# Weight loads issued by ScalarE instead of SyncE, and cache copies in rows of at most 4,096 bytes

## The chip, the core and the metric

The kernel runs on one core of a Trainium2 chip, in one launch. The metric is device time in microseconds from launch to end, the median of the runs. The core has TensorE (PE, matmuls), VectorE (DVE), ScalarE (ACT), GpSimd (POOL) and SyncE (SP, which issues DMAs and waits), each with an instruction stream of its own, tied by semaphores. SP, ACT and POOL can each issue DMAs; 16 DMA engines, shared by all, carry them out. Times in profiles are microseconds from the start of the span; "ns" is written where it is nanoseconds.

## The reference

One inference step of a two-layer decoder trunk, for a prompt of 256 tokens and for 8 sequences of 4 new tokens behind 2048 cached ones (288 token columns together). Each layer computes, in float32:

```
xn = rms_norm(x) * norm_w
p  = xn @ w_in                      # 35 tiles of 128 columns
a  = top-k sparse attention (indexer scores over 2048 cached keys, paged K and V)
c  = dilated sliding-window attention (windows 128, 512, 2048; dilations 1, 4, 16)
b  = Mamba-2 SSD branch (causal conv, chunked scan, state of 8 sequences)
h  = x + concat(a * silu(g_a), c * silu(g_c), b) @ w_out     # 8 tiles
```

The outputs are both normalised streams, the new keys and values, the SSD and conv states, and the window caches of each sequence moved on by 4 rows. For the last of these a cache of 128, 512 or 2048 rows is read from HBM and all but its first 4 rows are written to an output: 124, 508 and 2044 KB for each of 8 sequences and 2 layers, a plain copy that nothing in the kernel waits for until its end.

## The kernel before, in words

Everything is feature-major: x is 8 tiles of 128 features by 288 columns. The weights of a layer are 43 tiles of 512 KB (128 partitions by 4 KB), 35 for `w_in` and 8 for `w_out`; `w` in SBUF holds four of them (`WSLOTS`), so tile n + 4 can be loaded once PE has finished tile n. PE computes a tile as 8 products over k, each two instructions in the profile (line 825), into one of two PSUM banks; ACT (`evac`) or DVE (for the first three tiles of a layer, `LATE_ROOT`) moves the result to SBUF. There is no scheduler: each engine's order is written out by hand in its block, and semaphores `filled<bank>` and `drained<bank>` tie a tile's last matmul to its eviction, and that to the next use of the bank (`bank_plan`).

The layer goes through stages that the profile shows well:

- start: sum of squares of x, tiles 0 to 7.
- page stage: 16 page pairs (`page_pair`), each from two ring slots, with tiles 8 to 15 in between. A page load (`kv<-in_kk`) has 128 rows of 1,280 bytes.
- copy stage: tiles 16 to 26, between them the counting passes of the top-k threshold on DVE (`hit`) and the SSD heads. POOL issues the 24 cache copies here (`keep`), three after each of the tiles 16 to 21, 23 and 24.
- value stage: tiles 27 to 34 with windows (`kv<-in_dil`, 576 KB) and value pages (`kv<-in_vv`, 128 rows of 1,024 bytes).
- output: the 8 tiles of `w_out`, then the next layer's sum of squares.

Pages, windows and values pass through a ring of eight slots of `kv`. Loads of even places of the ring are issued by SP, of odd places by POOL, each when PE has used the item eight places before (`load_item`, line 404 for pages, 397 for windows). SP also issues every weight load (`load_w`, line 425), in `next_w(i)`: it waits until tile i is filled, then loads tile i + 4. SP's program interleaves these with the ring's loads in the order in which PE will release them. ACT issues no DMA. POOL's DMAs go through the queue that the profile calls q0, software_dynamic, SP's through q1, hardware_dynamic.

Of the kernel before, what the change touches and what calls it, by code (L numbers as in the profile page):

```python
# [23 lines left out]
DEPTH = 2  # L24
# [185 lines left out]
def build(nc, a):  # L210

    plan, _ = bank_plan()
    with ExitStack() as ctx:
# [103 lines left out]
        def filled(use):  # L317
            return S[f"filled{plan[use][0]}"]
# [101 lines left out]
        def _(sync):  # L420
            SP = mybir.EngineType.SP

            def load_w(layer, i):
                n = layer * NW + i
                sync.dma_start(w[:, n % WSLOTS, :, :].rearrange("p k n -> p (k n)"),
                               a["w"][n // NW, n % NW]).then_inc(S[f"w_in{n % WSLOTS}"], 16)

# [3 lines left out]
            load_w(0, 0)  # L431
            sync.dma_start(ptab[:, :], a["ptab"]).then_inc(S["ptab_in"], 16)
            load_w(0, 1)
            load_w(0, 2)
            sync.dma_start(const[:, :], a["const"]).then_inc(S["const_in"], 16)
            load_w(0, 3)
# [6 lines left out]
            for L in range(DEPTH):  # L443

                def next_w(i):


                    n = L * NW + i + WSLOTS
                    if n < DEPTH * NW:
                        use = f"proj{i}" if i < NTILE else f"out{i - NTILE}"  # L450
                        sync.wait_ge(filled(use), nth(L, use))
                        load_w(0, n)

# [5 lines left out]
                for i in range(8):  # L459
                    next_w(i)  # L460
                for u in range(NPAIR):
                    consumed(("page", 2 * u), ("page", 2 * u + 1))
                    if u % 2 == 1:
                        next_w(8 + u // 2)
# [3 lines left out]
                for i in range(16, 27):  # L468
                    next_w(i)
                for i, (lo, hi) in enumerate(((32, 40), (40, 44), (44, 46), (46, 54), (54, 62), (62, 66), (66, 70), (70, 74))):  # L470
                    consumed(*RING[lo:hi])
                    next_w(27 + i)
                consumed(*RING[74:])
                for m in range(KT):
                    next_w(NTILE + m)
# [7 lines left out]
        def _(pool):  # L483
# [5 lines left out]
            for L in range(DEPTH):  # L489
                ly = bass.ds(L, 1)  # L490

                def keep(b, use):

                    pool.wait_ge(filled(use), nth(L, use))
                    for g in range(3):
                        pool.dma_start(a[f"keep{g}"][ly, b], a[f"buf{g}"][ly, b, 4 * 256:]).then_inc(S["copied"], 16)  # L496
# [75 lines left out]
        def _(act):  # L572
            act.wait_ge(S["ones_set"], 1)
# [19 lines left out]
            for L in range(DEPTH):  # L593
                chain = Chain(S["act_chain"])

                def evac(i):
# [18 lines left out]
                    else:  # L615
                        act.activation(ptile(i), src[:, 0:T], fn).then_inc(use, 1)  # L616

# [74 lines left out]

                if L == 0:
# [119 lines left out]
                for k in range(KT):  # L813
                    square(L + 1, k)
# [1377 lines left out]
```

## Time and profile before

| | |
|---|---|
| runs | 687.83, 688.44, 694.17 us; median 688.44 |
| span of the profiled execution | 683.4 us, first to last instruction |
| that execution's own time | not given beside its span; the median of the runs lies 5.0 us above the span |
| PE busy | 614.2 us, 90% of the span |
| DVE, ACT, POOL busy | 377.5, 167.9, 224.5 us |
| DMA | 198.38 MB, mean 290 GB/s |
| mean granted TensorE clock | 0.957 of full |
| weight loads | 86 of 512 KB, 7.6 us to landing in the median |
| cache copies | 48: 16 each of 124, 508 and 2044 KB |

The page gives each engine's busy time, a strip of 40 slices, the chain of work that ended last, the costliest groups of instructions, and for each kind of DMA the median time from issue to landing. A PE wait is attributed to what released it; a chain of waits gives the whole length of a transfer, however much of it lies beside other work. A DMA's share is that of the 16 engines' time; it can come out a little over 1 in a short stretch, since a packet counts where it starts.

### The profile page before, as it was taken

To read this page: it belongs to the slowest core of one execution; us is meant where nothing else is said; L and a number is where in the kernel's file an instruction comes from. 1 tells how busy PE (TensorE), PEld (TensorE's weight loads), DVE (VectorE), ACT (ScalarE), POOL (GpSimd) and SP (SyncE) were. 2 spreads that over 40 slices of the span, in tenths; PEclk is the share of its full clock that TensorE was granted. 3 is DMA by queue.
4 is the path that set the end of the run, shared out by engine and by line. 5 is a ranking of instruction groups with operands and counts; after the bars stand their busy time and mean duration, and the time that the engine had idled before them with its cause. 6 is when DMAs were issued, how large, how long until landed. Compare 5 with 4: busy or idle time off the path is not lost.

```text
span 683.4 us, 13785 instructions
## 1 busy us (share of the span) xinstructions
PE 614.2 (90%) x4870; PEld 428.3 (63%) x4870; DVE 377.5 (55%) x1150; ACT 167.9 (25%) x405; POOL 224.5 (33%) x406
## 2 busy tenths in 40 slices
PE   6899999898989978979999999988899997898994
PEld 3676565565667755647777665566656775565772
DVE  3754655777759535433147475577766953543213
ACT  3015322121113202550111352312211320235111
POOL 2207540242106675451000475123120667541000
PEclk9999999998889998999999999999989999799897
DMA  8939999999978899995333799999998889993111
GB/s 333 374 133 315 367 369 408 418 346 356 350 246 270 308 315 371 351 293 204 113 115 141 263 369 369 395 408 376 367 361 297 276 307 310 371 332 121 54 69 69
DMA packets 67766, 198.38 MB, mean 290 GB/s; under 512 B 11537, under 2 KB 40370, under 8 KB 66418
## 3 DMA queue, kind: packets, MB, share of 16 engines
q1 hardware_dynamic: 49682, 99.99, 41.6%
q0 software_dynamic: 18016, 97.50, 39.7%
q8 instruction: 39, 0.64, 0.4%
q14 instruction: 29, 0.24, 0.1%
HBM read 189.30 MB, written 52.00 MB: 353 GB/s over the span
## 4 chain that ended last, share of the span: by engine, by line
PE 57%; DMA 18%; DVE 14%; SPq 4%; ACT 4%; issue 3%; DVEq 0%; ACTq 0%
PE bank L825 55%; DMA w<-in_w 6%; DMA kv<-in_kk 6%; DMA kv<-in_vv 5%; SPq L404 3%; DVE hit L1452 3%; PE bank L875 2%; DVE tb L1465 1%; DVE st L1954 1%; DMA ptab<-in_ptab 1%; ACT srow L766 1%; ACT shared L663 1%; DVE shared L1575 1%; ACT shared L680 1%; DVE tb L1463 1%
## 5 line engine op out<-in xcount | busy, mean ns | idle before, releaser
L825 PE MATMUL bank<-xn,w 128*128 128x288 f32 x1120 | 304.2, 426 | 4.7 <-DMA w<-in_w 4.7
L825 PEld LDWEIGHTS bank<-xn,w 128*128 128x128 f32 x1120 | 212.3, 197 | 78.4 <-issue 17.4
L404 POOL DMA_DIRECT2D kv<-in_kk x128 | 68.8, 538 | 153.6 <-issue 98.1
L404 POOL DMA_DIRECT2D kv<-in_vv x160 | 86.4, 540 | 99.3 <-PE bank L825 72.7
L616 ACT ACTIVATE pt<-bank 128x288 f32<-128x288 f32 x48 | 19.6, 409 | 237.7 <-PE bank L825 237.7
L825 PE MATMUL bank<-pt,w 128*128 128x288 f32 x256 | 65.2, 410 | 0.0
L825 PEld LDWEIGHTS bank<-pt,w 128*128 128x128 f32 x256 | 48.8, 192 | 14.1 <-issue 0.7
L496 POOL DMA_DIRECT2D out_keep<-in_buf x48 | 23.5, 495 | 81.3 <-PE bank L825 73.3
L825 PE MATMUL bank<-kv,pt 128*32 128x256 f32 x512 | 38.2, 406 | 11.5 <-DMA kv<-in_vv 11.3
L1452 DVE TENSOR_SCALAR_CACHE_REDUCE hit<-sc,tb 128x516 bf16<-128x516 f32 x62 | 46.5, 750 | 2.2
L2022 DVE TENSOR_TENSOR x<-x,bank 128x288 f32<-128x288 f32 x16 | 7.3, 454 | 50.2 <-PE bank L825 50.1
L825 PE MATMUL bank<-kv,qz 128*32 128x256 f32 x512 | 34.3, 385 | 0.0
L1463 DVE TENSOR_SCALAR tb<-bank 128x1 int32<-128x1 f32 x62 | 9.5, 154 | 42.5 <-PE bank L825 42.1
L1425 DVE COPY tails<-cin 128x3 f32<-128x3 f32 x14 | 7.2, 512 | 41.3 <-ACT cin L614 39.1
L825 PEld LDWEIGHTS bank<-cnt,seg 128*128 128x128 f16 x68 | 6.7, 100 | 35.9 <-issue 34.0
L825 PE MATMUL bank<-cnt,seg 128*128 128x1 f16 x68 | 11.1, 168 | 19.5 <-DVE hit L1452 18.8
L825 PEld LDWEIGHTS bank<-kv,pt 128*32 128x32 f32 x512 | 13.9, 112 | 22.4 <-DMA kv<-in_vv 10.1
L583 ACT ACTIVATE phased<-x 128x288 f32<-128x288 f32 x24 | 10.5, 442 | 70.6 <-DVE x L2022 67.6
L825 PE MATMUL bank<-kv,shared 128*32 128x128 f32 x768 | 26.6, 283 | 0.0
L825 PE MATMUL bank<-pt 64*128 64x128 f32 (+3 forms) x168 | 26.3, 334 | 0.0
L518 POOL TENSOR_SCALAR xwb<-xws,const 32x384 f32<-32x384 f32 x16 | 21.6, 1354 | 13.4 <-DVE xws L1715 7.6
L825 PEld LDWEIGHTS bank<-pt 64*128 64x128 f32 (+2 forms) x168 | 17.9, 183 | 10.6 <-issue 9.8
(238 smaller groups left out, 802.8 us busy)
## 6 DMA issues: line engine op xcount, KB each, us to landing
w<-in_w SPq DMA_DIRECT2D x86, 512.0 KB, 7.6
out_keep<-in_buf POOLq DMA_DIRECT2D x16, 2044.0 KB, 14.3
kv<-in_kk SPq DMA_DIRECT2D x128, 160.0 KB, 8.8
kv<-in_kk POOLq DMA_DIRECT2D x128, 160.0 KB, 5.8
kv<-in_vv POOLq DMA_DIRECT2D x160, 128.0 KB, 5.3
kv<-in_dil SPq DMA_DIRECT2D x24, 576.0 KB, 8.2
kv<-in_vv SPq DMA_DIRECT2D x96, 128.0 KB, 5.1
out_keep<-in_buf POOLq DMA_DIRECT2D x16, 508.0 KB, 8.8
```

Source lines behind the costliest of these rows:

```text
L404: engine.dma_start(kv[:, s, r * rec:(r + 1) * rec], a["kk" if what == "page" else "vv"][bass.ds(page + layer * N_POOL, 1)].rearrange("o p ...
L496: pool.dma_start(a[f"keep{g}"][ly, b], a[f"buf{g}"][ly, b, 4 * 256:]).then_inc(S["copied"], 16)
L518: pool.tensor_scalar(xwb[:, b % 2, :], xws[0:32, 2, :], C("bm", b, b + 1, slice(0, 32)), None, ALU.mult).then_inc(S["xwb_ready"], 1)
L583: act.activation(squares[:, k % 2, 0:T], x[:, k, :], ACT.Square).then_inc(S["sq_ready"], 1)
L616: act.activation(ptile(i), src[:, 0:T], fn).then_inc(use, 1)
L663: act.activation(psa[:, i, 0:nk], psa[:, i, 0:nk], ACT.Exp, bias=st8[:, 1, i:i + 1], accum_out=st8[:, 2, i:i + 1]).then_inc(S["pexp"] if i ...
L825: return pe.matmul(out, lhsT, rhs, start=start, stop=stop, skip_group_check=True, **k)
L875: return pe.transpose(out, in_, ident(n))
L1425: dve.tensor_copy(tails[:, n, 0:3], cin[:, n % 2, TP:TP + 3]).then_inc(chain.next(), 1)
L1452: ts_(hit[:, :], sc[:, :], old.bitcast(F32), 0.0, ALU.is_ge, ALU.add, accum_out=cnt[:, 0:1]).then_inc(S["cnt_ready"], 1)
L1463: ts_(tb[:, 2:3], src[:, 0:1], float(TOPK_S), float(bit), ALU.is_lt, ALU.mult).then_inc(drained(f"count{n}"), 1)
L2022: tt_(x[:, m, :], x[:, m, :], src[:, 0:T], ALU.add).then_inc(drained(f"out{m}"), 1)
```

## The change

ACT issues all weight loads. The first four come before anything else in its program; the next three behind the first root, and each later one directly behind the eviction of the tile whose slot it refills (`next_w(i)` at the end of `evac(i)`; for the output tiles ahead of `square`). SP keeps x, the parameters, the constants, the even places of the ring and the state. The copies get `max_dma_last_dim=4096`, which cuts each into equal rows of at most 4,096 bytes.

```diff
@@ block.sync
-            def load_w(layer, i):
-                n = layer * NW + i
-                sync.dma_start(w[:, n % WSLOTS, :, :].rearrange("p k n -> p (k n)"),
-                               a["w"][n // NW, n % NW]).then_inc(S[f"w_in{n % WSLOTS}"], 16)
-
             for n in range(2):
                 sync.dma_start(x[:, 4 * n:4 * n + 4, :], a["x"][:, 4 * n:4 * n + 4, :]).then_inc(S[f"x_in{n}"], 16)
             sync.dma_start(prm[:, :, :], a["prm"]).then_inc(S["prm_in"], 16)
-            load_w(0, 0)
             sync.dma_start(ptab[:, :], a["ptab"]).then_inc(S["ptab_in"], 16)
-            load_w(0, 1)
-            load_w(0, 2)
             sync.dma_start(const[:, :], a["const"]).then_inc(S["const_in"], 16)
-            load_w(0, 3)
...
-                for i in range(8):
-                    next_w(i)
                 for u in range(NPAIR):
                     consumed(("page", 2 * u), ("page", 2 * u + 1))
-                    if u % 2 == 1:
-                        next_w(8 + u // 2)
...
-                for i in range(16, 27):
-                    next_w(i)
-                for i, (lo, hi) in enumerate(((32, 40), (40, 44), (44, 46), (46, 54), (54, 62), (62, 66), (66, 70), (70, 74))):
-                    consumed(*RING[lo:hi])
-                    next_w(27 + i)
-                consumed(*RING[74:])
-                for m in range(KT):
-                    next_w(NTILE + m)
+                consumed(*RING[32:])
@@ block.gpsimd, keep(b, use)
-                        pool.dma_start(a[f"keep{g}"][ly, b], a[f"buf{g}"][ly, b, 4 * 256:]).then_inc(S["copied"], 16)
+                        pool.dma_start(a[f"keep{g}"][ly, b], a[f"buf{g}"][ly, b, 4 * 256:], max_dma_last_dim=4096).then_inc(S["copied"], 16)
@@ block.scalar
+            def load_w(n):
+
+                act.dma_start(w[:, n % WSLOTS, :, :].rearrange("p k n -> p (k n)"),
+                              a["w"][n // NW, n % NW]).then_inc(S[f"w_in{n % WSLOTS}"], 16)
+
+            for n in range(WSLOTS):
+                load_w(n)
             act.wait_ge(S["ones_set"], 1)
...
+                def next_w(i):
+
+                    n = L * NW + i + WSLOTS
+                    if n < DEPTH * NW:
+                        use = f"proj{i}" if i < NTILE else f"out{i - NTILE}"
+                        act.wait_ge(filled(use), nth(L, use))
+                        load_w(n)
...
                     else:
                         act.activation(ptile(i), src[:, 0:T], fn).then_inc(use, 1)
+                    next_w(i)
...
+                for i in range(LATE_ROOT):
+                    next_w(i)
...
                 for k in range(KT):
+                    next_w(NTILE + k)
                     square(L + 1, k)
```

SP at the start of the program, before, from its second instruction on; `w<-in_w` is a weight tile, `x`, `prm`, `ptab`, `const`, `cst`, `bconst` and `fnw` are the other first loads:

```order
L429 DMA x<-in_x 128x1152 x2
L430 DMA prm<-in_prm 128x102
L425 DMA w<-in_w 128x1024
L432 DMA ptab<-in_ptab 1x256
L425 DMA w<-in_w 128x1024 x2
L435 DMA const<-in_const 128x1844
L425 DMA w<-in_w 128x1024
L437 DMA cst<-in_conv 128x336
L439 DMA bconst<-in_bconst 128x1932
L439 DMA fnw<-in_fnw 128x8
L400 TENSOR_LOAD ptab
```

The same place of SP in the change:

```order
L424 DMA x<-in_x 128x1152 x2
L425 DMA prm<-in_prm 128x102
L426 DMA ptab<-in_ptab 1x256
L427 DMA const<-in_const 128x1844
L428 DMA cst<-in_conv 128x336
L430 DMA bconst<-in_bconst 128x1932
L430 DMA fnw<-in_fnw 128x8
L400 TENSOR_LOAD ptab
```

ACT at the start of the program in the change (`phased` holds the squares, `pt` the evicted tiles); before, it had the same rows without the DMAs:

```order
L542 UNCONDITIONAL_BRANCH
L546 DMA w<-in_w 128x1024 x4
L561 ACT_TABLE_LOAD
L561 ACTIVATE phased<-x 128x288 x8
L566 ACT_TABLE_LOAD
L566 ACTIVATE rstd<-bank,eps 128x288
L546 DMA w<-in_w 128x1024 x3
L602 ACTIVATE pt<-bank 128x288
L546 DMA w<-in_w 128x1024
L591 ACTIVATE misc<-bank 64x288
L592 ACTIVATE pt<-bank 64x288
L546 DMA w<-in_w 128x1024
```

The four first weight tiles have moved from between SP's loads to the head of ACT's program, the next three behind the root (`rstd`), and the others each behind the eviction of its tile.

SP in the middle of the page stage, before, where one page item ends and the next begins; `ptab` is the load of page numbers into registers:

```order
L404 ISA
L404 DMA kv<-in_kk 128x320
L404 ISA
L404 DMA kv<-in_kk 128x320
L404 ISA
L404 DMA kv<-in_kk 128x320
L425 DMA w<-in_w 128x1024
L400 TENSOR_LOAD ptab
L404 ISA
```

ACT behind the eviction of tile 28, in the change (`vtok` are the turned value tiles, of which PE waits for `drained`):

```order
L602 ACT_TABLE_LOAD
L602 ACTIVATE pt<-bank 128x288
L546 DMA w<-in_w 128x1024
L643 ACTIVATE vtok<-bank 128x384 x2
L643 ACTIVATE vtok<-bank 32x384
L771 ACTIVATE shared<-bank 128x32x2 x3
L775 ACTIVATE ea<-bank 32x384
```

On SP the weight load between two page items is gone, so that only page loads follow each other; on ACT a weight load now stands between an eviction and what followed it directly.

POOL at the first `keep`, before:

```order
L397 DMA kv<-in_dil 128x1152 x4
L513 DMA out_tails<-tails 128x189
L496 DMA out_keep<-in_buf 16x1984
L496 DMA out_keep<-in_buf 16x8128
L496 DMA out_keep<-in_buf 32x16352
L500 DMA out_feat<-pt 128x288
L500 DMA out_feat<-pt 128x576
```

The same in the change:

```order
L397 DMA kv<-in_dil 128x1152 x4
L484 DMA out_tails<-tails 128x189
L467 DMA out_keep<-in_buf 32x992
L467 DMA out_keep<-in_buf 128x1016
L467 DMA out_keep<-in_buf 512x1022
L471 DMA out_feat<-pt 128x288
L471 DMA out_feat<-pt 128x576
```

The order is the same; the three copies have 32, 128 and 512 rows of 3,968, 4,064 and 4,088 bytes where they had 16, 16 and 32 rows of 7,936, 32,512 and 65,408. (The order's rows count elements of 4 bytes.)

## Rows read from the trace of the kernel before

**Rows 1.** the page: busy us, share of the span, instructions, by engine

```profile
PE 614.2 (90%) x4870; PEld 428.3 (63%) x4870; DVE 377.5 (55%) x1150; ACT 167.9 (25%) x405; POOL 224.5 (33%) x406
```

**Rows 2.** busy us in stretches: page stage, both layers' starts, copy stage

```profile
49.50:116.40 66.90, 65.40 (x693) 39.19 (x693) 37.07 (x118) 23.93 (x61) 31.01 (x54) 1.00 1.01 360
13.10:53.00 39.90, 35.98 (x218) 26.46 (x216) 25.27 (x76) 5.18 (x13) 8.63 (x18) 1.00 0.72 257
344.30:381.50 37.20, 36.65 (x221) 27.26 (x220) 25.61 (x76) 6.16 (x14) 0.56 (x2) 1.00 0.37 129
121.50:198.50 77.00, 66.42 (x382) 47.29 (x383) 53.63 (x203) 14.16 (x43) 18.27 (x40) 0.93 1.00 363
```

**Rows 3.** the waits of PE: us in total, times, longest

```profile
PE bank L825 <- DMA kv<-in_vv: 11.3, 8, 2.9
...
PE bank L825 <- DMA w<-in_w: 4.7, 2, 3.4
PE bank L825 <- DMA kv<-in_kk: 2.3, 4, 0.9
PE bank L875 <- ACT vtok L656: 1.4, 4, 0.5
PE bank L875 <- ACT pt L773: 1.3, 4, 0.4
...
PE bank L825 <- ACT relun L700: 1.1, 2, 0.6
```

**Rows 4.** chain of waits, end of the copy stage: start, us, what

```profile
163.77 34.05 DMA w<-in_w
...
197.86 6.00 PE bank L825 x18
```

**Rows 5.** tile x: the two loads' issues, and us from issue to landing

```profile
L429 SPq DMA_DIRECT2D x<-in_x x2: 391/406/421, 0.9 to 1.3; - x2
...
DMA to landing us min/median/max: 3.8/4.3/4.8
```

**Rows 6.** SP's timeline at the start: when the seven next weight loads begin

```profile
21.92 23.34 SPq L425 DMA_DIRECT2D w<-in_w  x7
```

**Rows 7.** PE's timeline at the start

```profile
32.19 8.03 PE L825 MATMUL bank<-xn,w 128*128 128x288 f32 x32 [3.37 <-DMA w<-in_w]
```

**Rows 8.** DMA queues between 81 and 83: packets, MB, share of 16 engines

```profile
q0 software_dynamic: 152, 0.52, 73.0%
q1 hardware_dynamic: 160, 0.21, 31.2%
```

**Rows 9.** chain of waits of the page stage: start, us, what

```profile
95.26 13.64 DMA kv<-in_kk
```

**Rows 10.** SP's timeline in the page stage: start, us, what

```profile
97.30 0.34 SPq L425 DMA_DIRECT2D w<-in_w  x1
...
105.19 0.33 SPq L425 DMA_DIRECT2D w<-in_w  x1
```

**Rows 11.** DMA queues between 158 and 175: packets, MB, share

```profile
q0 software_dynamic: 219, 5.15, 83.4%
q1 hardware_dynamic: 219, 0.77, 14.4%
```

**Rows 12.** stretches as in rows 2, PE alone

```profile
198.00:201.40 3.40, 3.40 (x8) 0.50 0.49 182
201.40:210.00 8.60, 8.35 (x170) 1.00 0.28 94
524.00:529.00 5.00, 4.75 (x26) 1.00 0.47 166
```

**Rows 13.** PE's timeline in the second layer's value stage

```profile
595.79 1.07 PE L825 MATMUL bank<-kv,pt 128*32 128x256 f32 x16 [1.90 <-DMA kv<-in_vv]
```

**Rows 14.** all weight loads: issue ns min/median/max, then us to landing

```profile
L425 SPq DMA_DIRECT2D w<-in_w x86: 327/328/1615, 2.3 to 654.3; - x86
...
DMA to landing us min/median/max: 3.3/7.6/34.0
```

More of the change, by code:

```diff
@@ L443, in _ @@
             for L in range(DEPTH):
[L445 to L452, printed above, removed]
                 def consumed(*items):
```

## The prediction, made before the change was run

> **What bounds the kernel now.** I read the page first: TensorE (PE) is busy 614.2 us of the 683.4 us span, in 4870 matmuls, and no other engine comes near [rows 1]. The change touches no matmul and no eviction, so it can only move PE's idle time, some 69 us, and the clock that PE is granted. Next the busy time by stage [rows 2]: a row has the stretch, its length, the busy us of PE, weight loads, DVE, ACT and POOL with counts, the granted clock, the DMA engines' share and GB/s. In the page stage (49.5 to 116.4) PE idles 1.5 us of 66.9, with the DMA engines at 1.01: PE and DMA are both full. The copy stage (121.5 to 198.5) again has DMA at 1.00, while PE idles for other reasons. Then the waits of PE [rows 3]: 11.3 us for value pages (kv<-in_vv), 4.7 us for weights, 2.3 us for key pages (kv<-in_kk). The 86 weight loads cost PE 4.7 us in all, though the chain of waits puts one of 34.05 us on the path [rows 4]: that row is the length of a transfer, 33 us of it beside PE's own work. So what the weights can win is small, and what the other loads can lose by sharing must be weighed against it.
>
> **Term 1, the first loads.** SP's queue had x, the parameters and then four weight tiles; now ACT issues the four tiles at once, beside x. The two halves of x (576 KB each) are issued 0.9 and 1.3 us in and land 3.8 and 4.8 us later [rows 5], so at 4.7 and 6.1: the second takes 1.4 us at the full rate. If the weights take every second turn, the first half needs 1.4 us more. PE's first sum of squares waits for it, and the first tiles follow. I take **+1.4 us**; bounds 0 (x gets ahead) and +2.9 (both halves late and both on the path).
>
> **Term 2, tile 4.** Its load stood on SP behind 16 page loads and left at 21.92 [rows 6]; PE was ready at 28.8 and waited 3.37 us for it [rows 7]. On ACT it leaves once tile 0 is filled, three tiles of 4.0 us before that, near 17, and has over 10 us to land. The whole wait is not won: DVE and ACT then become the next. The second layer's same eight tiles have no such wait and take 37.2 us where the first takes 39.9 [rows 2]. I take the difference, **-2.7 us**; bounds -3.4 and -1.0.
>
> **Term 3, the page stage.** Here the queue matters. Between 81 and 83 the software queue (POOL) had 152 packets and 0.52 MB, the hardware queue (SP) 160 packets and 0.21 MB [rows 8]: they alternate packet by packet, and the bigger packet gets the bigger share. SP's pages of 1,280-byte rows are the losers. In SP's own queue the weights stood in line with them; from a queue of their own, with 4 KB packets, they take a turn in each round, ahead of pages that were issued earlier. The last SP page load leaves at 95.26 and lands 13.64 us later, and PE goes on with it [rows 9]. Two weight loads leave meanwhile, at 97.30 and 105.19 [rows 10]; before, they stood behind that page. Now the first, 512 KB at the 360 GB/s of this stage [rows 2], puts 1.5 us in front of it, the second, with some 2 us of its transfer left, a third of a share, 0.6 us at most. The engines were full already, so the page lands later by that. I take 1.6 us a layer, the first load and little of the second: **+3.2 us** for both layers. Bounds: -2.3 (the waits for pages vanish) and +4.0.
>
> **Term 4, the copy stage.** The cache copies moved in pieces of up to 65,408 bytes, and now move in pieces of at most 4,096. Between 158 and 175 each queue had 219 packets, the copies 5.15 MB, the weights 0.77 MB [rows 11]: one for one again. Each engine has 8 weight rows of a tile, and each waits for one copy packet. That is why the load of tile 26 took 34.05 us and PE started on it only at 197.86 [rows 4]. With equal packets it should land in some 6 us. The wait was 4.7 less 3.37, so 1.3 us. Behind it the clock fell to 0.50 for 3.4 us [rows 12], the lower of its levels, 1.2 GHz; the same tile of the second layer, with no wait ahead, kept 1.00. Half of 3.4 us is 1.7. **-3.0 us**, all in the first layer; bounds -3.0 and 0 (the threshold count on DVE is next on this path, and the clock can fall elsewhere).
>
> The Trainium skill speaks against this term: its page "DMA: Bandwidth & Descriptors", section "Queues, rings and completion order", has a DMA engine drain a whole packet of typically 9 to 17 descriptors from one row's ring before it turns to the next. By that all 8 rows of a weight tile would pass behind a single copy packet, the copies' size would not matter, and the sum would be 3.0 us higher, 693.1. The trace's 219 to 219 and the 34 us disagree with it.
>
> **Term 5, the copies themselves.** 24 copies a layer, 21.9 MB. In the first window above the copies had 83.4% of 16 engines over 17 us for 5.15 MB, 22.7 GB/s an engine; POOL's small packets [rows 8] make 22.2, SP's 21.0. So smaller rows make 60 us of copying 1 to 5 us longer, which lies in the stretch after 201.4, where the engines are at 0.28 [rows 12]: **0**. If that room were gone, up to 5 us a layer would appear at the value pages. POOL's issue instructions may grow; its pages wait for PE there, not for POOL.
>
> **Term 6, the value stage.** PE waits 11.3 us for value pages [rows 3], and the last wait of the second layer, 1.90 us, is for an SP load [rows 13]. Tile 35's load leaves in front of it and now competes. One load is worth 1.5 us, as in term 3; part of it has no time to interfere. I take 0.6 us a layer, **+1.2 us**; bounds 0 and +3.0.
>
> **Term 7, ACT's issues.** An issue takes SP 327 ns at least, 328 in the median, 1,615 at most [rows 14]. ACT makes 82 behind evictions; the eviction itself is not delayed, what comes after it on ACT is. PE waits for such work at `relun`, for the turned weights `pt` and for `vtok` [rows 3], eight places in all where a new issue lies just before. Bounds: 0 (the issue runs while ACT still computes) and 8 x 0.33 = +2.6. I take 0.2 each, **+1.6 us**.
>
> **Sum:** 1.4 - 2.7 + 3.2 - 3.0 + 0 + 1.2 + 1.6 = +1.7 us against the profiled execution. Its span is 683.4 us; the median, 688.44, lies 5.0 above it, which nothing here changes. Forecast **690.1 us**.
>
> **Rivals.**
>
> *The queue is neutral.* Weights on ACT's queue take nothing from the pages; they only leave the line in front of them. For it: POOL's share can shrink instead of SP's. Against it: the alternation in [rows 8]. Then term 3 is -1.5 and term 6 is 0: 1.4 - 2.7 - 1.5 - 3.0 + 1.6 = -4.2, so 684.2 us. The same page of the skill, section "Issuing engines are not separate DMA queues", says that issuing from another engine saves only the sequencer's time; by that rule it would be this case.
>
> *ACT is held by its issues (slower).* SP's issues reach 1,615 ns where its queue is deep. If ACT's meet that at the eight places of term 7, each costs 1.3 us instead of 0.2: +8.8, so 698.9 us. It decides from about 1 us an issue. Against it: ACT has at most four loads in flight, SP up to sixteen.
>
> *The copies overrun (slower).* If a 4 KB packet between two places of HBM took 1.5 times its share, the copying would last 30 us longer, POOL's value pages would stand behind it in the same queue, and after some 20 us of room PE would wait 10 us a layer: 710 us. It needs 1.35 times; the nearest rows say 1.08 at most.
>
> *The value stage speeds up too (faster).* SP's queue loses its heaviest rows, the waits for in_vv [rows 3] shrink by a third, and a spell of half clock as the first in [rows 12] goes in each layer: the neutral case less 3.8 and less 2 x 1.7, so 677 us.
>
> **Chances.** The forecast's mechanisms 0.50, with their own range of 686 to 695; the neutral queue 0.28; ACT held 0.08; copies overrun 0.05; value stage faster 0.06; something else 0.03. The forecast's low bounds and the neutral case set the low end, 683.0; term 3 at its upper end, the upper bounds of 1, 6 and 7 and most of the held ACT set the high end, 697.5. Outside lie the fast rival, the overrun and the tails, 0.2 together. About 1%, 6.9 us, is what a measurement of this kernel can tell from no change. Faster than 681.6: the fast rival and a tail of the neutral case, 0.13. Slower than 695.3: both slow rivals and a tail of the forecast, 0.20. Within: 0.67.
>
> **What the profile of the changed kernel would show.** Term 1: the second half of x lands near 9 instead of 6.1, tile 0 starts near 14.5. Term 2: no wait of PE at tile 4. Term 3: page-stage weights land in 5 to 7 us, SP's last pages later than 13.64 us after issue, and PE's waits for in_kk above 2.3 us; if they are gone, the neutral rival holds. Term 4: no weight load over 12 us, tile 26 without a wait and at full clock. Term 5: small packets in q0, its last copy before 207. Term 7: waits for `relun`, `pt` and `vtok` 0.2 us longer each. What would make the forecast wrong is a stage whose time moves by more than 3 us, above all the value stage, or spells of half clock that come or go without a wait beside them.

## The result, and the profile after

The changed kernel takes **800.02 us** (median of 4 runs, 796.93 to 803.46), the kernel before 691.11 us beside it: a ratio of 1.157, 95% interval 1.150 to 1.165. 690.1 was forecast, with a range up to 697.5. The prediction was wrong by 110 us. A kernel's runs fall into a faster and a slower state of the chip, some per cent apart: times here are medians of all runs, ratios compare fast runs only, and of the profiled executions those of experiments 16, 17 and 18 were slow ones.

The profiled execution has a span of 795.3 us against 683.4. Busy time by engine, from the page, to set beside [rows 1]:

```profile
PE 628.7 (79%) x4870; PEld 435.9 (55%) x4870; DVE 378.2 (48%) x1150; ACT 169.7 (21%) x405; POOL 228.1 (29%) x406
```

The instructions are the same, and only PE's busy time grew, by 14.5 us. The rest is waiting. PE's waits, with total, times and longest (compare [rows 3]):

```profile
PE bank L815 <- DMA kv<-in_vv: 93.8, 13, 28.3
...
PE bank L815 <- issue: 8.4, 4, 4.6
...
PE bank L815 <- DMA kv<-in_kk: 6.5, 5, 1.8
PE bank L815 <- DMA w<-in_w: 5.1, 2, 3.8
PE bank L865 <- ACT pt L762: 2.5, 3, 1.1
PE bank L865 <- ACT vtok L643: 1.7, 4, 0.5
PE bank L815 <- ACT relun L689: 1.1, 2, 0.5
```

The waits for value pages grew from 11.3 to 93.8 us, 82.5 of the 111.9 us. With PE's extra busy time and the 8.4 us of "issue" (waits that end in nothing the profile shows) that makes 105. Four waits are 79.4 of the 93.8 us, on PE's timeline (start, length, what, and in brackets the idle time ahead):

```profile
254.74 1.08 PE L815 MATMUL bank<-kv,pt 128*32 128x256 f32 x8 [18.31 <-DMA kv<-in_vv]
284.12 1.94 PE L815 MATMUL bank<-kv,pt 128*32 128x256 f32 x16 [28.30 <-DMA kv<-in_vv]
635.74 1.08 PE L815 MATMUL bank<-kv,pt 128*32 128x256 f32 x8 [11.96 <-DMA kv<-in_vv]
657.65 1.94 PE L815 MATMUL bank<-kv,pt 128*32 128x256 f32 x16 [20.84 <-DMA kv<-in_vv]
```

The issues of these pages began in time, at 212.9 (207.5 before). These are the loads issued from 214 to 223, with the median time to landing:

```profile
kv<-in_vv POOLq DMA_DIRECT2D x12, 128.0 KB, 48.7
kv<-in_vv SPq DMA_DIRECT2D x8, 128.0 KB, 33.8
```

Before, the median over all such loads was 5.3 us on POOL's queue and 5.1 on SP's. Both queues are late, not only POOL's, in which the copies stand. The page that POOL issued at 217.5 landed 66.6 us later, at 284.1, where the longest of the four waits ends; SP's of 215.2 landed 39.4 us later, at 254.6, where the wait of 18.31 us ends. What is ahead of them are the copies of the first layer, last issued at about 187: ns of an issue and the first and last issue, then us from issue to landing:

```profile
L467 POOL DMA_DIRECT2D out_keep<-in_buf x48: 503/532/631, 121.8 to 585.1; - x48
...
DMA to landing us min/median/max: 4.2/49.2/94.3
```

Before, the median was 10.8 us and the longest 23.8. The last copy of the first layer was issued at 187.0 and took the 94.3 us, so it landed at 281.3, and 3 us later the longest wait of PE ends. Stretches as in [rows 2] (us, busy us by engine, granted clock, DMA share, GB/s) show it from both sides:

```profile
49.50:116.40 66.90, 63.42 (x656) 38.04 (x655) 35.43 (x114) 24.04 (x61) 31.02 (x54) 1.00 1.01 363
13.10:53.00 39.90, 39.27 (x229) 29.02 (x230) 25.89 (x78) 7.56 (x17) 10.07 (x19) 1.00 0.77 265
121.00:198.00 77.00, 65.97 (x366) 46.33 (x364) 52.20 (x199) 14.98 (x43) 19.73 (x40) 0.91 1.06 211
198.00:240.00 42.00, 28.29 (x307) 21.98 (x306) 23.69 (x69) 8.45 (x15) 12.04 (x19) 0.77 1.02 209
240.00:300.00 60.00, 15.11 (x90) 8.95 (x91) 2.99 (x6) 2.55 (x8) 7.18 (x10) 0.57 0.67 202
```

Up to 116 the kernels agree within 2 us. In the copy stage PE still does its work (65.97 of 77 us), and the DMA engines are as full as before (1.06), but they move **211 GB/s where they moved 363** [rows 2]. A full engine with 60% of its bytes is the sign to look for: its packets take longer, though not all of them. The trace's packet records, which the views only sum, show which: between 130 and 190 half of ACT's weight packets of 4,096 bytes took 159 ns, in the change as in experiment 3 below, but the slowest tenth took 995 ns and more for 170, and the mean was 386 for 173. Of the copies' packets of 8,176 bytes the median was 455 ns, the mean 696 and the slowest tenth over 1,478; in experiment 6, with packets of the same size, 311, 374 and 521. So a part of the packets is held up for long, and that part makes most of the loss. The bill comes after 198. Of 234.1 to 292.1, which lies around the two waits, PE computes 9.78 us, at the lower clock throughout:

```profile
234.10:292.10 58.00, 9.78 (x48) 5.23 (x49) 3.41 (x16) 3.13 (x6) 4.62 (x9) 0.50 0.74 219
```

Last, the DMA queues from 158 to 175, to set beside [rows 11] (packets, MB, share of 16 engines; q10 is ACT's):

```profile
q0 software_dynamic: 266, 1.90, 62.7%
q10 hardware_dynamic: 261, 0.97, 43.4%
```

The copies' 1.90 MB in 62.7% of 16 engines over 17 us are 11.1 GB/s an engine, against 22.7 before: 2.04 times the time for a byte. ACT's weight rows, at 8.2 GB/s an engine, suffer too, though their rows are 4,096 bytes as before.

### The profile page after: what moved, and what is told of

It is laid out like the page before. It is cut to its first block, busy times and chain, and to the rows that moved or that the text cites. A ratio compares the mean times of both kernels' runs of the same rounds, so it can differ in the third digit from the quotient of the medians.

```text
span 795.3 us, 13785 instructions
## 1 busy us (share of the span) xinstructions
PE 628.7 (79%) x4870; PEld 435.9 (55%) x4870; DVE 378.2 (48%) x1150; ACT 169.7 (21%) x405; POOL 228.1 (29%) x406
## 4 chain that ended last, share of the span: by engine, by line
PE 54%; DMA 25%; DVE 9%; another core or an unknown queue 4%; issue 3%; ACT 2%; SPq 2%; POOLq 0%; DVEq 0%; ACTq 0%; POOL 0%
PE bank L815 52%; DMA kv<-in_vv 14%; DMA kv<-in_kk 5%; DMA w<-in_w 5%; DVE hit L1442 2%; PE bank L865 2%; SPq L404 2%; DVE tb L1455 1%; DMA x<-in_x 1%; ACT shared L650 1%; DVE shared L1565 0%; ACT shared L667 0%; DVE st L1571 0%; DVE tb L1453 0%
## 5 line engine op out<-in xcount | busy, mean ns | idle before, releaser
L815 PE MATMUL bank<-xn,w 128*128 128x288 f32 x1120 | 310.6, 433 | 5.1 <-DMA w<-in_w 5.1
L815 PEld LDWEIGHTS bank<-xn,w 128*128 128x128 f32 x1120 | 216.7, 201 | 82.2 <-issue 19.0
L815 PE MATMUL bank<-kv,pt 128*32 128x256 f32 x512 | 42.4, 436 | 93.8 <-DMA kv<-in_vv 93.8
L404 POOL DMA_DIRECT2D kv<-in_kk x128 | 69.1, 540 | 158.0 <-issue 94.4
L1754 DVE TENSOR_TENSOR phased<-phased,ebc 128x384 f32<-128x384 f32 x16 | 9.0, 560 | 115.1 <-PE bank L815 115.1
L467 POOL DMA_DIRECT2D out_keep<-in_buf x48 | 26.5, 557 | 82.2 <-PE bank L815 80.4
L815 PE MATMUL bank<-kv,shared 128*32 128x128 f32 x768 | 31.1, 307 | 8.2 <-issue 8.2
L815 PEld LDWEIGHTS bank<-kv,shared 128*32 128x32 f32 x768 | 24.9, 124 | 13.4 <-issue 11.0
L815 PEld LDWEIGHTS bank<-cnt,seg 128*128 128x128 f16 x68 | 6.7, 101 | 35.8 <-issue 33.8
## 6 DMA issues: line engine op xcount, KB each, us to landing
kv<-in_vv SPq DMA_DIRECT2D x96, 128.0 KB, 11.1
```

The source lines that it names most:

```text
L404: engine.dma_start(kv[:, s, r * rec:(r + 1) * rec], a["kk" if what == "page" else "vv"][bass.ds(page + layer * N_POOL, 1)].rearrange("o p ...
L815: return pe.matmul(out, lhsT, rhs, start=start, stop=stop, skip_group_check=True, **k)
L1754: tt_(state[:, b, :].rearrange("p (h n) -> p h n", h=6), state[:, b, :].rearrange("p (h n) -> p h n", h=6), each(ebc[:, :, 2 + b], 64), AL ...
```

## The experiments

The rate of the DMA engines between 130 and 190, in the first layer's copy stage, is the common measure: the engines are full there (share 0.98 to 1.07) in every kernel. It is the last number of the row of that stretch. In every experiment whose time stays under 710 us the same stretch of the second layer, 460 to 520, gives the same within 7 GB/s. Experiments 3 and 16 have the same copies and gave 368 and 357, so a difference of 11 between two kernels is not read as one. The last column is the ratio of times to the kernel before, which ran beside each experiment anew (medians of 687.8 to 691.1 us), with its 95% interval.

| | copy pieces | starts off a 32-byte multiple | GB/s | us | ratio |
|---|---|---|---|---|---|
| before | 65,408 | none | 355 | | 1 |
| change | 4,088 end to end | 3 of 4 | 199 | 800.0 | 1.157 (1.150, 1.165) |
| 1 | 65,408, old copies | none | 358 | 690.9 | 1.006 (1.002, 1.010) |
| 2 | 4,088, weights on SP | 3 of 4 | 225 | 779.3 | 1.136 (1.127, 1.145) |
| 3 | 4,096 | none | 368 | 689.6 | 1.003 (0.998, 1.008) |
| 4 | 65,400 | 3 of 4 | 338 | 690.2 | 1.005 (1.001, 1.009) |
| 5 | 4,032 | none | 362 | 688.0 | 1.004 (1.000, 1.009) |
| 6 | 4,088, 8 bytes apart | none | 356 | 689.5 | 1.005 (1.000, 1.010) |
| 7 | 4,096, read at +8 | reads only | 363 | 693.6 | 1.014 (1.004, 1.023) |
| 8 | 4,096, written at +8 | writes only | 312 | 701.0 | 1.025 (1.016, 1.034) |
| 9 | 4,096, both at +8 | all | 306 | 701.2 | 1.017 (1.014, 1.021) |
| 10 | 4,104 end to end | 3 of 4 | 221 | 788.7 | 1.142 (1.138, 1.146) |
| 11 | 4,032, both at +8 | all | 331 | 694.6 | 1.008 (1.003, 1.012) |
| 12 | 4,064 | none | 364 | 689.8 | 0.999 (0.994, 1.004) |
| 13 | 4,096, both at +24 | all | 305 | 706.3 | 1.023 (1.015, 1.031) |
| 14 | 4,080 | 1 of 2 | 334 | 697.4 | 1.013 (1.007, 1.020) |
| 15 | 8,184 | 3 of 4 | 328 | 699.2 | 1.017 (1.010, 1.024) |
| 16 | as 3, first weights on SP | none | 357 | 687.1 | 0.999 (0.995, 1.004) |
| 17 | 4,088, 8 bytes apart, both at +8 | all, no shared unit | 357 | 690.3 | 0.999 (0.994, 1.005) |
| 18 | 4,088, read apart, written end to end | writes only, 3 of 4 | 220 | 782.6 | 1.129 (1.116, 1.142) |

The piece of 4,088 bytes is what a limit of 4,096 makes of a cache of 2,093,056 bytes: 512 equal pieces of 8 x 511. The smaller caches got 4,064 and 3,968. The trace shows the sizes: packets of 8,176 bytes, two rows each. Within its tensor every cache begins at a multiple of 4,096 bytes. "Starts off a 32-byte multiple" is counted from there, for the largest cache, on the written side where nothing else is said; the other two caches hold a quarter of the bytes, and in the change their rows of 4,064 and 3,968 bytes are multiples of 32.

**Experiment 1: the weights alone.** The changed kernel with the old copies.

```diff
-  pool.dma_start(a[f"keep{g}"][ly, b], a[f"buf{g}"][ly, b, 4 * 256:], max_dma_last_dim=4096)
+  pool.dma_start(a[f"keep{g}"][ly, b], a[f"buf{g}"][ly, b, 4 * 256:])
```

> Weight loads on ACT as in the change, copies in their old pieces of up to 65,408 bytes. Theories that blame the copies (their piece size, or where the pieces start) expect the other terms of the forecast alone: first loads +1.9 (measured in the changed kernel), tile 4 -2.7, pages +3.2, values +1.2, issues 0.3, so near 693 us, between 686 and 697, with the last copy of layer 0 landed before 200 us and the loads of the copy stage taking up to 34 us as before. The theory that a queue of ACT's own for the weights is what slows the DMA engines expects over 740 us and copies that land after 240 us.

690.93 us. A queue of ACT's own is not the cause of the loss. This kernel carries the other terms of the forecast and is read for them below.

**Experiment 2: the copies alone.** The kernel before with only the edit of the copies.

> Weight loads on SP as before, copies in pieces of at most 4,096 bytes (4,088 in fact). Both theories of the copies expect the whole loss: 800 us, 785 to 815, copies landing near 280 us. The theory of ACT's queue expects 688 to 700 us.

779.31 us. The edit of the copies is the cause. That it is 20 us less than the whole change is more than the other terms give; with ACT's loads beside them the copies move at 199 GB/s, with SP's at 225.

**Experiment 3: 4,096 bytes exactly.** Same size within 8 bytes, other borders.

```diff
+  keep, buf, n = a[f"keep{g}"][ly, b], a[f"buf{g}"][ly, b, 4 * 256:], (WINS[g] - 4) * 256
+  m = 1024
+  r = n // m // 16 * 16
+  for lo, hi, k in ((0, r * m, r), (r * m, n, 16)):
+      pool.dma_start(keep[:, lo:hi].rearrange("o (k e) -> o k e", k=k), buf[:, lo:hi].rearrange("o (k e) -> o k e", k=k), max_dma_last_dim=4096)
```

> The changed kernel with the same bytes copied in pieces of 4,096 bytes, each of which starts at a multiple of 4,096 (the last 61,440 bytes of each cache in 16 pieces of 3,840), in place of 4,088. Theory alignment (4,088 is 8 x 511, so nearly every piece begins and ends inside a 64-byte line, and the partial lines cost): near the kernel of experiment 1, 690 to 700 us. Theory piece size (any piece near 4 KB between two places of HBM is dear): 785 to 815 us. In between, 720 to 760, would mean that both count.

689.61 us: the whole loss is gone with 8 bytes more in a piece, so pieces near 4 KB are not dear as such. The copies' queue between 158 and 175, as above:

```profile
q0 software_dynamic: 1465, 5.23, 84.7%
q10 hardware_dynamic: 292, 1.05, 16.1%
```

That is 22.7 GB/s an engine, the same as with 65,408 bytes. Nor does any weight load stand behind a copy now (ns of an issue, then us to landing; before the longest was 34.0, [rows 14]):

```profile
L550 ACTq DMA_DIRECT2D w<-in_w x86: 333/334/983, 0.9 to 654.8; - x86
...
DMA to landing us min/median/max: 3.3/6.5/12.2
```

**Experiment 4: large pieces at odd places.** 65,400 bytes in place of 65,408.

> Weight loads on ACT; copies in large pieces that start at odd places: 65,400 bytes for the largest cache in place of 65,408 (8 x 8,175), 32,496 and 7,920 for the others, the few bytes left over in 16 small pieces. Theory piece size: as experiment 1, within 3 us. Theory alignment by edges (a price for each piece's two ends): a sixteenth of the loss, 7 us over experiment 1. Theory alignment of the whole piece (every burst of a displaced piece is split): 750 us and more.

690.21 us: 20 GB/s less than with 65,408 in the stage (340 for 358 in the second layer too), nothing in the time. That rules out a price by the byte, and it fits a price at the borders, of which there are a sixteenth.

**Experiments 5, 12 and 14: the grid.** Pieces of 4,032, 4,064 and 4,080 bytes end to end, written as in experiment 3 with m = 1008, 1016, 1020; the starts are multiples of 64, 32 and 16.

> The changed kernel with copy pieces of 4,032 bytes (63 x 64), the rest of each cache in 16 pieces, all starts and lengths multiples of 64 bytes but not of 128. Two such rows make one packet, as with 4,088 bytes. Theory partial 64-byte lines: as the 4,096-byte pieces, 686 to 695 us. Theory that a larger unit counts (128 to 512 bytes, or the 4,096 itself), or that the pairs of rows in a packet are what is dear: 740 us and more.

> Pieces of 4,064 bytes (127 x 32), two rows a packet, undisplaced: every second start lies 32 bytes inside a 64-byte line, the others on it. If 64-byte lines count, half of the borders are unaligned against 7 of 8 with 4,088 bytes: 4/7 of the 110 us, near 750 us. If the unit is 32 bytes: 686 to 695 us.

> Pieces of 4,080 bytes (255 x 16), two rows a packet, undisplaced: starts drift over 0, 16, 32, 48 in a line. If only starts that are no multiple of 16 are dear: 686 to 695 us. If the unit is 32 bytes, half of the starts are off it, against three quarters with 4,088: about 760 us (2/3 of the loss). If the drift is what counts, whatever the unit: 760 to 800.

362, 364 and 334 GB/s. Multiples of 64 and of 32 are free, those of 16 lose 8%, with half of the borders inside a 32-byte unit. So the unit is 32 bytes, not the 64 that the expectation of experiment 3 named. But 4,080 costs far less than two thirds of the loss.

**Experiments 6 and 17: off the grid, but no unit shared.** Pieces of 4,088 bytes at a stride of 4,096, with the 8 bytes left out at the end (6) or at the start (17). The lines are those of 6; in 17 both sides begin 8 bytes further, and the last 61,184 bytes of the largest cache go end to end in 16 pieces of 3,824.

```diff
+  dst = keep[:, lo:lo + k * m].rearrange("o (k e) -> o k e", k=k)[:, :, 0:used]
+  src = buf[:, lo:lo + k * m].rearrange("o (k e) -> o k e", k=k)[:, :, 0:used]
```

> Pieces that start at multiples of 4,096 bytes, but only the first 4,088 of each are copied (8 of 4,096 bytes are left out), so every piece ends inside a line, and no line is written by two pieces. Theory of the partial line by itself (the memory has to read and merge it): half of the partial lines are left, so half of the loss or more, 730 to 800 us. Theory of the shared line (two pieces, on two DMA engines, write the same line at about the same time and wait for one another): 686 to 695 us.

> The mirror of experiment 6: pieces of 4,088 bytes at a stride of 4,096 on both sides, each starting 8 bytes behind a multiple of 4,096 and ending on one (8 of 4,096 bytes, and 256 bytes of each cache, are left out). No line is shared by two pieces. Theory that the dear pieces are those whose start and end lie differently (every second one with 4,088 bytes packed): under 250 GB/s in the copy stage and 760 us and more. Theory shared lines: 350 GB/s or more, 686 to 695 us. Theory of a fixed price for a start off the grid: 305 to 330 GB/s, 695 to 706 us.

356 and 357 GB/s, what experiment 16 gives with aligned pieces, and no change of the time. A piece with one end inside a unit costs nothing that can be measured, where one of the theories put it at half of the loss or more. Both kernels keep the stride of 4,096 bytes, so they take away the wandering of the starts together with the shared unit, and none of these pieces has both ends inside a unit.

**Experiments 7, 8 and 9: which side.** Pieces of 4,096 bytes, displaced by 8 bytes in the reads, the writes, or both. The lines are those of 8.

```diff
+  dst = keep[:, lo + 2:lo + 2 + k * m].rearrange("o (k e) -> o k e", k=k)
+  src = buf[:, lo + 0:lo + 0 + k * m].rearrange("o (k e) -> o k e", k=k)
```

> Pieces of 4,096 bytes written at multiples of 4,096, read from 8 bytes further (so the copied caches are displaced by 8 bytes, and the last 1,024 bytes of each stay out). Theory that the writes are what costs: 686 to 695 us. Theory that reads at odd places cost: most of the 110 us.

> The mirror of the last: pieces of 4,096 bytes read at multiples of 4,096 and written 8 bytes further (displaced, last 1,024 bytes left out). Theory of the writes: two pieces share a line at every border, as in the changed kernel, with 496 borders in place of 512: 785 to 810 us. Theory of the reads: 686 to 695 us.

> Pieces of 4,096 bytes read and written 8 bytes behind a multiple of 4,096 (the first 8 and the last 1,016 bytes of each cache are left out). Reading alone displaced gave 693.6 us, writing alone 701.0, the changed kernel 800. Theory that the two sides add: near 705 us. Theory that a piece displaced on both sides is what is dear: 780 us and more. Theory that it is the drift of the starts over all places in a line, or the two rows in a packet, which this kernel has not: up to 710 us.

363, 312 and 306 GB/s. Displaced reads do not slow the stage; the time of experiment 7, 1.4% up in four runs (interval 0.4 to 2.3%), is not explained by its rate, and whether it is a loss stays unclear. Displaced writes, where each border now lies inside a unit that two pieces write, take 15 to 17%. The stretch 130 to 190 of experiment 9:

```profile
130.00:190.00 60.00, 53.35 (x301) 37.76 (x301) 42.16 (x159) 12.31 (x35) 26.01 (x54) 0.91 1.04 306
```

PE's 53.35 us there are as good as the 53.12 of experiment 3 and the 51.95 of the change: it is not this stage that shows the damage. The theory of the writes had put experiment 8 at 785 us or more, and it measured 84 less: a shared unit at every border is not yet what the change has.

**Experiments 10 and 11: wandering starts, or two rows in a packet.** 4,104 bytes end to end (one row a packet), and 4,032 bytes all displaced by 8 (two rows a packet).

> Pieces of 4,104 bytes (8 x 513), one row a packet, whose starts drift by 8 bytes from row to row as those of the changed kernel do the other way. Theory drift: near 800 us. Theory that two rows in a packet of the queue are what is dear together with odd starts: 700 to 715 us.

> Pieces of 4,032 bytes (63 x 64), two rows a packet, all of them displaced by the same 8 bytes on both sides (the first 8 and up to 248 last bytes of each cache are left out). Undisplaced they gave 688.0 us. Theory that two rows in a packet with odd starts are dear (the line between the two rows of one packet is written twice by one engine in quick succession): 780 to 800 us. Theory drift: 700 to 715 us.

221 and 331 GB/s. Two rows in a packet are not what is dear; starts that wander by 8 bytes, in pieces of this length, are.

**Experiment 13: 24 bytes in place of 8.**

> As experiment 9, with a displacement of 24 bytes in place of 8 on both sides (the first 24 and the last 1,000 bytes of each cache are left out). If every place off the 32-byte grid costs the same, as with 8 bytes: 695 to 705 us. If the place counts, and those deeper in a unit are the dear ones: 760 us and more. If neither, the drift itself is what is dear (neighbouring pieces with different remainders), and this gives 695 to 705 too.

305 GB/s, as with 8. Of these two places within the unit, neither is dearer.

**Experiment 15: pieces twice as long, still wandering by 8 bytes.**

> Pieces of 8,184 bytes (8 x 1,023) for the two larger caches: the same drift of 8 bytes, half as many borders. A price for each piece: half the extra time of the DMA engines, and since the stage has some 20 us of room a layer before PE waits, 700 to 745 us. A price by the byte (a displaced piece moves slower throughout): 780 us and more.

328 GB/s and 699.2 us: not a price by the byte. But neither is it a fixed price for each border: half the borders of experiment 10 give back 90 of its 100 us, and 107 of the 147 GB/s that it lacks to experiment 3.

**Experiment 18: wandering writes, fixed reads.**

```diff
+  dst = keep[:, 0:r * 1022].rearrange("o (k e) -> o k e", k=r)[:, :, 0:1022]
+  src = buf[:, 0:r * 1024].rearrange("o (k e) -> o k e", k=r)[:, :, 0:1022]
```

> Pieces of 4,088 bytes read at a stride of 4,096 from multiples of 4,096, and written end to end at a stride of 4,088 (so they are displaced, and 8 of 4,096 bytes are left out). Theory that the drift of the written places alone is what is dear: 199 to 230 GB/s in the copy stage, 770 to 800 us. Theory that the read side is needed too, or that both must drift together: 300 GB/s and more, under 710 us.

220 GB/s, 782.6 us. The writes alone are enough for nearly all of the loss.

**Experiment 16: the change without its loss, first loads in their old order.** The first four weight tiles go back to SP behind x; the copies are those of experiment 3.

> Aligned pieces of 4,096 bytes and the weights on ACT, but the first four weight tiles on SP behind x, in the order of the kernel before. It takes term 1 out (tile 0 of the first layer started 2.2 us later in experiments 1 and 3). Expected 2 us under experiment 3: a ratio to the kernel before of 0.995 to 1.002, so no change that can be measured; anything under 0.990 would mean that the lateness of x costs more than its 2.2 us.

687.11 us, 0.999 (0.995, 1.004). No version here beats the kernel before by more than can be measured.

**What is shown, and what is open.** Shown: the loss comes from the borders between the written pieces. With borders at multiples of 32 bytes it is gone (3, 5, 12, 16), with 8 bytes between pieces at a stride of 4,096 too (6, 17); where the copies read from does not matter to the rate (7, 18). Fixed borders inside a 32-byte unit that two pieces write cost 9 to 17% of the rate (11 beside 5, 9 and 13 beside 3), and half as many, at starts that wander by 16 bytes, 8% (14 beside 5). That it takes the unit shared by two neighbours, and not a partly written unit alone, is shown for fixed borders only as far as 6 and 17 go: no kernel here has both ends of a piece inside a unit without a neighbour in it. Open: why borders that wander in steps of 8 bytes cost 37% and more with pieces near 4 KB (2, 10, 18, the change), more than twice what fixed ones do, though fewer of them lie inside a unit, and why the same wandering costs only 11% with pieces of 8,184 bytes (15 beside 3) and 6% with 65,400 (4 beside 1). In all of these the pieces also share units; no kernel has wandering starts with gaps between the pieces, so that the shared unit is needed for this large part of the loss is argued and not shown. Lengths that are an odd multiple of 8 do not explain it by themselves (6 and 17 have them). That two DMA engines have to take turns for the unit they share fits all of this, and it fits the long tail of the packets, but no run shows which engine writes which piece.

## Why the prediction was wrong

**Term 5 failed**: "smaller rows make 60 us of copying 1 to 5 us longer", which it then put at 0. It measured 110 us: 800.0 for 689.6 in experiment 3, where only the cutting of the copies differs. From its first issue to its last landing the copying of the first layer took 159.5 us for 76.9. It was costed from the rates of the nearest rows, 22.7 GB/s an engine for the large copy pieces and 21 to 22 for page loads of 1,280-byte rows [rows 8, 11]. For size that was right: with 4,096 bytes the copies run at 22.7. But size was not what counts. The pieces of 4,088 bytes stood in the section on the change, and I did not ask where such pieces begin. None of the rows that I priced by could show it: the large copy pieces, of 7,936, 32,512 and 65,408 bytes, are all multiples of 32, and pages land in SBUF, each row in a partition of its own, while these copies tile one stretch of HBM end to end. The measured rate was 11.1 GB/s an engine.

The unit of 32 bytes stands in the Trainium skill, on its page "Collectives: The Full Stack", section "Rules for kernel authors": buffers, there those of collectives, are to be aligned to 32 bytes, to avoid a read-modify-write by the hardware. Experiments 5, 12 and 14 agree with the unit, by 362 and 364 GB/s for 334. But in experiments 6 and 17, with one partly written unit a piece and 356 and 357 GB/s, such a write costs nothing that can be measured.

**The room behind the copies** was judged rightly, and it decides the size of the loss. In the rival "the copies overrun" I put it at some 20 us a layer. In experiment 9, at 306 GB/s, the copying takes 20 and 16 us longer in the two layers than before, from first issue to last landing, and PE's waits for value pages grow only from 11.3 to 15.3 us in both together. In the change the copying takes 83 us longer in the first layer and 56 in the second, and the same waits grow by 50 and 32: some 33 and 24 us were free. In times: experiments 8, 9 and 13, at 305 to 312 GB/s, lose 1.7 to 2.5%; 14 and 15, at 334 and 328, lose 1.3 and 1.7%; the change, at 199, loses 15.7%. Of the 1.3 to 2.5% the waits for value pages show only a part (10.5 to 17.5 us in these five, 11.3 before); no run says where the rest lies.

That rival had the chain from the copies to the waits, but not the cause: it blamed the 4 KB packet, which experiment 3 clears. It needed 1.35 times the share and got 2.04. It was priced at 30 us of overrun, where the copying took 83 and 56 us longer, and at 10 us a layer, where PE waited 46.6 and 32.8 us in the four rows above. It also took only POOL's queue to be held; SP's value pages took 33.8 us too. What it left out is the clock: 14.5 us more busy time for the same 4,870 matmuls, at a mean granted clock of 0.892 for 0.957. With 0.05 for it, the chance was far too low for a price that no row of the trace bounded from above: the row that I took as the upper bound differed from the new operation in where it writes.

The other terms are read from experiment 1, whose span is 682.6 us against 683.4. PE's timeline at the start of tiles 0, 8, 16 and 27 of the first layer, then of tiles 8, 16 and 27 of the second:

```profile
15.29 0.41 PE L815 MATMUL bank<-xn,w 128*128 128x288 f32 x1
51.48 0.51 PE L815 MATMUL bank<-xn,w 128*128 128x288 f32 x1
115.87 0.51 PE L815 MATMUL bank<-xn,w 128*128 128x288 f32 x1
210.67 0.51 PE L815 MATMUL bank<-xn,w 128*128 128x288 f32 x1
380.73 0.51 PE L815 MATMUL bank<-xn,w 128*128 128x288 f32 x1
444.91 0.51 PE L815 MATMUL bank<-xn,w 128*128 128x288 f32 x1
539.35 0.51 PE L815 MATMUL bank<-xn,w 128*128 128x288 f32 x1
```

The kernel before has, at the same places:

```profile
13.13 0.41 PE L825 MATMUL bank<-xn,w 128*128 128x288 f32 x1
52.96 0.51 PE L825 MATMUL bank<-xn,w 128*128 128x288 f32 x1
116.36 0.51 PE L825 MATMUL bank<-xn,w 128*128 128x288 f32 x1
212.24 0.51 PE L825 MATMUL bank<-xn,w 128*128 128x288 f32 x1
381.51 0.51 PE L825 MATMUL bank<-xn,w 128*128 128x288 f32 x1
444.20 0.51 PE L825 MATMUL bank<-xn,w 128*128 128x288 f32 x1
536.86 0.51 PE L825 MATMUL bank<-xn,w 128*128 128x288 f32 x1
```

- **Term 1** (+1.4): tile 0 starts 2.2 us later, within the bounds, and PE's first wait, for the squares of x, is 8.6 us for 6.7.
- **Term 2** (-2.7): from tile 0 to tile 8 it took 39.83 us and takes 36.19, so -3.6, a little beyond the bound of -3.4. PE has no wait for a weight tile there.
- **Term 3** (+3.2): from tile 8 to tile 16, 63.40 and 62.69 us became 64.39 and 64.18, +2.5 in both layers together. The weights do take turns from the pages: tile 15 of the first layer lands 6.5 us after its issue for 13.3 before, PE's waits for in_kk grow from 2.3 to 4.8 us, by the same 2.5, and the longest is 2.6 us for 0.9. They grow in experiment 3 and in the change too, to 5.3 and 6.5. The neutral rival, by which they do not grow, is wrong here.
- **Term 4** (-3.0): in experiment 1 nothing of it can be there. In experiment 3 the loads of this stage land within 12.2 us, as forecast for small pieces, and from tile 16 to tile 27 the two layers take 94.0 and 92.5 us, for 94.8 and 94.4 in experiment 1: -2.7. Against the kernel before (95.9 and 92.7) it is -2.0. PE's waits for weights, 4.7 us before and 1.6 in experiment 1, are gone. The size stays open: the term was forecast for the first layer alone, where it is -0.8 beside experiment 1 and -1.9 beside the kernel before. The 1.7 us that it took from the clock are not seen: over 116.5 to 210 the granted clock was 0.93 before, in experiment 1 and in experiment 3. In the changed kernel itself the term failed with term 5: the load that left at 165.50 took 37.53 us, because the rows it alternates with had become slow.
- **Term 6** (+1.2): from tile 27 of the second layer to the end, 683.4 - 536.9 = 146.5 us before and 143.3 in experiment 1. It went the other way, -3.3, and from tile 27 of the first layer to tile 8 of the second it is +0.8. The waits for value pages grew from 11.3 to 12.0 us. Tiles 16 to 27, where experiment 1 has the old copies, moved by -1.1 and +1.8 between the same two executions, so a stage's time is not known to 2 us from them and the size of this term stays open.
- **Term 7** (+1.6): an issue takes ACT 334 ns, and the waits for `vtok` went from 1.4 to 1.7 us, for `relun` not at all. +0.3; the issues lie beside ACT's other idle time. No issue of ACT's took more than 784 ns in experiment 1, so the rival "ACT held" is wrong.

So moving the weights was a trade of a few us, as forecast: a ratio of 1.006 (1.002 to 1.010), 1 to 7 us, where the terms without 4 and 5 sum to 4.7. The two profiled executions differ by -0.8, so single ones settle a term of 1 us as little as the sum. Experiment 3, with every term but the loss, measures 1.003 (0.998 to 1.008), which holds both no change and the forecast of 1.002.

The prediction weighed a rule against term 4, from the Trainium skill's page "DMA: Bandwidth & Descriptors", section "Queues, rings and completion order": a whole packet of typically 9 to 17 descriptors drains before the turn changes, which would have kept the weight loads slow behind copies of any size. Experiment 3, with 12.2 us as the longest weight load, disagrees with that size of a packet: there a copy packet is one row of 4,096 bytes.

## What to carry to other kernels

A limit on the size of the pieces sets where they begin: divide the copied length by hand and look whether the starts are multiples of 32 bytes, and cut off a tail rather than let an even division pick an odd length. Where the DMA engines are full, read GB/s beside their share; a full engine that moves less has packets that are held up, and no lack of work. And a copy that nobody waits for still has a room: ask what is issued behind it on its engines, and how much longer it may run before that is late. Here 16 to 20 us a layer nearly vanished in front of the waits behind them (experiment 9), and of 83 us 50 came back (the change).

## What the runs showed of the hardware

- Copies between two places of HBM cost the same for a byte in rows of 4,096 and of 65,408 bytes: 22.7 GB/s a DMA engine for both, beside weight loads.
- Rows written end to end whose borders are no multiple of 32 bytes are slower: all borders displaced by the same 8 or 24 bytes, 305 to 306 GB/s for 368; borders that wander by 8 bytes, 199 to 225 with pieces of 4,088 and 4,104 bytes, 328 with 8,184, 338 with 65,400. Rows of 4,088 bytes with 8 bytes between them: 356 and 357.
- While such copies run, the packets of other queues on the same DMA engines are slow too: weight rows of 4,096 bytes moved at 0.97 MB in 43.4% of 16 engines over 17 us, 8.2 GB/s an engine, against 1.05 MB in 16.1%, 24 GB/s, in experiment 3. Half of these packets took 159 ns in both; the slowest tenth took 995 ns and more for 170.
- PE was granted 0.50 for 58.0 us around two waits of 18.3 and 28.3 us in which it did nothing: the lower of its two levels, 1.2 GHz.
